# A hybrid decoder layer on one core: the delta rule's queries, keys and values turned by DMAs and VectorE instead of TensorE

## What is computed

```python
(gla_q, gla_k, gla_v, gla_lr, gla_r, gdn_qkv, gdn_b, gdn_a, gdn_z,
 xa_q, gate_logits) = jnp.split(u @ w_in, idx, axis=-1)
...
qkv = causal_short_conv(gdn_qkv, gdn_conv)      # 4 taps along the tokens, then SiLU
q, k, v = jnp.split(qkv, [GDN_QK, 2 * GDN_QK], axis=-1)
q = l2norm(q...) * (GDN_DK ** -0.5);  k = l2norm(k...)
o = gdn_chunked(q, k, v, g, beta)               # 8 heads of 128, chunks with a triangular solve
o = rmsnorm(o, gdn_norm) * jax.nn.silu(gdn_z...)
y_gdn = o @ w_up_gdn
```

## Time and profile before

| | |
|---|---|
| median of 3 runs (lowest to highest) | 2496.83 us (2495.46 to 2498.13) |
| the profiled execution | 2495.89 us, its span 2494.2 us |
| busy: PE, PEld, DVE, ACT, POOL | 99%, 82%, 56%, 50%, 17% |
| L676, the matmuls of the stream | 86% of the chain that ended last |
| DMA | 498.53 MB, 200 GB/s on the mean |
| `nat<-nat`, DMAs that exchange quarters | x416, 32 KB each, 3.7 us to landing |

### The profile page before, as it was taken

The page is one execution under the profiler, slowest core; times in us unless marked ns, Lnnn a source line. Parts: engine busy times, 40 slices in busy tenths (PEclk is TensorE's granted clock), DMA queues, the critical chain, the costliest instruction groups (busy, mean ns, idle before and its releaser), DMA issues.

```text
span 2494.2 us, 32008 instructions
## 1 busy us (share of the span) xinstructions
PE 2467.6 (99%) x11197; PEld 2044.4 (82%) x11197; DVE 1397.4 (56%) x1698; ACT 1235.8 (50%) x1502; POOL 430.8 (17%) x853
## 2 busy tenths in 40 slices
PE   9999999999999999999999999999999999999998
PEld 7888888888888888888888888888888888888887
DVE  5555555555556456676676564465655555555444
ACT  6444444444445456757585444444644444444443
POOL 6212121122101003223231120010121211211000
PEclk9999999999999999999999999999999999999999
DMA  7777677677768656555564766765676776767654
GB/s 251 211 201 210 202 208 203 202 214 210 215 211 266 195 171 171 167 161 163 158 178 135 215 207 196 225 221 187 215 211 200 204 206 201 210 201 252 194 190 157
DMA packets 305838, 498.53 MB, mean 200 GB/s; under 512 B 28236, under 2 KB 102096, under 8 KB 304976
## 3 DMA queue, kind: packets, MB, share of 16 engines
q1 hardware_dynamic: 282336, 457.85, 61.7%
q0 software_dynamic: 23120, 38.95, 4.9%
q10 hardware_dynamic: 288, 0.52, 0.1%
HBM read 471.39 MB, written 8.52 MB: 192 GB/s over the span
## 4 chain that ended last, share of the span: by engine, by line
PE 91%; POOL 2%; DVE 2%; DMA 2%; ACT 2%; issue 1%; SPq 0%; DVEq 0%; POOLq 0%; ACTq 0%
PE acc L676 86%; POOL mkh L636 1%; POOL mkh L639 1%; PE acc L718 1%; PE acc L701 1%; DMA post_a<-n_ffn_post 1%; DMA sq<-mk_scratch 1%; DVE wlo L1580 1%; ACT whi L1105 0%; DMA raw<-w_ffn_gu 0%; PE mix L736 0%; PE mix L945 0%; DMA raw<-w_in 0%; PE mix L839 0%; PE mix L979 0%
## 5 line engine op out<-in xcount | busy, mean ns | idle before, releaser
L1580 DVE TENSOR_TENSOR wlo<-raw,whi 128x1024 fp32r<-128x1024 f32 x860 | 1052.1, 1228 | 898.6 <-ACT whi L1105 895.3
L1105 ACT ACTIVATE whi<-raw 128x1024 fp32r<-128x1024 f32 x860 | 909.8, 1060 | 1177.2 <-PE acc L676 1134.7
L676 PE MATMUL acc<-whi,x_hi 128*128 128x512 f32 x1616 | 629.6, 390 | 0.0
L676 PE MATMUL acc<-whi,x_lo 128*128 128x512 f32 x1616 | 628.7, 389 | 0.0
L676 PE MATMUL acc<-wlo,x_hi 128*128 128x512 f32 x1616 | 628.7, 389 | 0.0
L676 PE MATMUL acc<-whi,u_hi 128*128 128x512 f32 x896 | 357.4, 399 | 1.9 <-ACT pr L1187 1.3
L676 PEld LDWEIGHTS acc<-whi,x_lo 128*128 128x128 f32 x1616 | 303.3, 188 | 63.2
L676 PEld LDWEIGHTS acc<-wlo,x_hi 128*128 128x128 f32 x1616 | 303.3, 188 | 62.7
L676 PEld LDWEIGHTS acc<-whi,x_hi 128*128 128x128 f32 x1616 | 303.3, 188 | 62.5
L300 POOL DMA_DIRECT2D nat<-nat x416 | 204.0, 498 | 848.4 <-DVE nat L1702 676.2
L676 PE MATMUL acc<-whi,u_lo 128*128 128x512 f32 x896 | 349.4, 390 | 0.0
(11 more groups left out here) (360 smaller groups left out, 1627.8 us busy)
## 6 DMA issues: line engine op xcount, KB each, us to landing
raw<-w_ffn_gu SPq DMA_DIRECT2D x352, 512.0 KB
raw<-w_ffn_down SPq DMA_DIRECT2D x176, 512.0 KB
raw<-w_in SPq DMA_DIRECT2D x224, 256.0 KB
raw<-w_in SPq DMA_DIRECT2D x96, 512.0 KB
raw<-w_mem_kv SPq DMA_DIRECT2D x32, 512.0 KB
raw<-w_out SPq DMA_DIRECT2D x32, 512.0 KB
nat<-nat POOLq DMA_DIRECT2D x416, 32.0 KB, 3.7
raw<-w_in SPq DMA_DIRECT2D x64, 128.0 KB
```

The costliest lines, as they stand in the source:

```text
L676: ins = nc.tensor.matmul(acc[:, par, t, :], x[:, k0 + k, cols], w[:, s, k, :], start=first and k == 0 and m == 0, stop=last and k == UK - ...
L1105: act(whi[:, s], raw[:, s], ACT.Copy).then_inc(hi_ready, 1)
L1580: tt(wlo[:, s], raw[:, s], whi[:, s].bitcast(fp32), ALU.subtract).then_inc(lo_ready, 1)
```

## The change

ScalarE now evicts chunks 0 and 1 by `take_in`: queries, keys and values go to `in_rows` with their columns in four quarters, in runs of 32 numbers; `z` goes to a place of its own (`z_in`, behind them in `pr`). For chunk 1 these are four instructions instead of two. GpSimd's new `swap_in(g)` waits for both evictions and exchanges quarters of partitions by 16 DMAs of 48 KB into `in_swapped`, which shares its place with `o_turned` and `o_swapped`. It is issued ahead of the loop for group 0 and at the end of the body for group g+1, behind the 30 instructions of the substitution. VectorE's new `turn_in(g)` in slot 25 waits for them and makes two block transposes of 128x768 into `x_in`, at the place of `in_rows`. The twelve transposes of L874 in each group are gone, with `gdn_in`; ScalarE seeds the convolution from `x_in` in SBUF, and VectorE's taps read `x_in` in SBUF instead of `mix` in PSUM. The evictions of the next chunks 0 and 1 wait for `conv_done`. TensorE's wait `groups_done` moves from step 0 to step 1.

```diff
+TURN_IN = STEP_AT.index(21)
...
+        flat = pr[:, 0:2, :, :].rearrange("p c t n -> p (c t n)")
+        in_rows, x_in = flat[:, 0:6 * SEQ], flat[:, 0:6 * SEQ].rearrange("p (k s) -> p k s", s=SEQ)
+        z_in = flat[:, 6 * SEQ:8 * SEQ].rearrange("p (t n) -> p t n", t=NT)
+        in_swapped = sums[:, :, :, :].rearrange("p c t n -> p (c t n)")[:, 0:6 * SEQ]
...
+            def swap_in(g):
+
+                for par in range(2):
+                    pl.wait_ge(acc_out[par], QB["proj"] // 2 + g * 2 + 1)
+                if g:
+                    pl.wait_ge(sem("in_turned"), g)
+                if g > 1:
+
+                    pl.wait_ge(sem("out_swapped"), 256 * (g - 1))
+                    pl.wait_ge(sem("out_lo"), g - 1)
+                for j in range(4):
+                    for q in range(4):
+                        pl.dma_start(in_swapped[32 * j:32 * j + 32, q * 384:(q + 1) * 384],
+                                     in_rows[32 * q:32 * q + 32, j * 384:(j + 1) * 384]).then_inc(sem("in_swapped"), 16)
+
+            swap_in(0)
             for g in range(NG):
...
                     pl.tensor_tensor(xcol[:, :, i + 1:], xcol[:, :, i + 1:], term[:, :, i + 1:], ALU.subtract).then_inc(sem("substituted"), 1)
+                if g + 1 < NG:
+                    swap_in(g + 1)
...
-                if j == 0:
+                if j == 1:
+
                     groups_done(pe, g)
-                    pe.wait_ge(acc_out[0], qp + g * 2 + 1)
-                    pe.wait_ge(acc_out[1], qp + g * 2 + 1)
-                    for b in range(3):
-                        for h in range(2):
-                            for t in range(NT):
-                                o = (b % 2) * 256 + h * P
-                                ins = nc.tensor.transpose(mix[:, b, h * SEQ + t * P:h * SEQ + (t + 1) * P],
-                                                          pr[:, b // 2, t, o:o + P], ident)
-                    ins.then_inc(sem("gdn_in"), 1)
...
+            def take_in(n, c):
+
+                ac.wait_ge(unit_used, n + 1)
+                v = in_rows.rearrange("p (j t k l) -> p t k j l", j=4, t=NT, l=32)
+                for t in range(NT):
+                    scale = rs[:, R_H1, t:t + 1]
+                    if c == 0:
+                        ins = act(v[:, t, 0:4], acc[:, 0, t, :].rearrange("p (k j l) -> p k j l", j=4, l=32), ACT.Copy, scale=scale)
+                    else:
+                        act(v[:, t, 4:6], acc[:, 1, t, 0:256].rearrange("p (k j l) -> p k j l", j=4, l=32), ACT.Copy, scale=scale)
+                        ins = act(z_in[:, t], acc[:, 1, t, 256:512], ACT.Copy, scale=scale)
+                ins.then_inc(acc_out[c], 1)
...
-                    need("gdn_in")
+                    need("in_turned")
...
-                            ins = act(conv[:, 2 * b + h, :], mix[:, b, h * SEQ:(h + 1) * SEQ], ACT.Copy,
+                            ins = act(conv[:, 2 * b + h, :], x_in[:, 2 * b + h, :], ACT.Copy,
...
-                    act(zg[:, :, :], pr[:, 1, :, 256:512], ACT.Silu)
+                    act(zg[:, :, :], z_in, ACT.Silu)
...
-                    for name in (("gdn_in",), ("gdn_in", "silu_zr"), ("gla_in", "gla_o"), ("xa_in", "silu_zr"))[c]:
+                    if c < 2:
+                        ac.wait_ge(sem("conv_done"), mixed * 3 + 3)
+                    for name in ((), ("silu_zr",), ("gla_in", "gla_o"), ("xa_in", "silu_zr"))[c]:
...
-                            ins = stt(y, mix[:, b, h * SEQ:(h + 1) * SEQ - s], cwg[:, 3 * (TAPS - 1 - s) + b, h:h + 1], y,
+                            ins = stt(y, x_in[:, 2 * b + h, 0:SEQ - s], cwg[:, 3 * (TAPS - 1 - s) + b, h:h + 1], y,
...
+            def turn_in(g):
+
+                ve.wait_ge(sem("in_swapped"), 256 * (g + 1))
+                src = in_swapped.rearrange("p (q t k l) -> p t k q l", q=4, t=NT, l=32)
+                dst = x_in.rearrange("p k (t q l) -> p t k q l", q=4, l=32)
+                for t in range(NT):
+                    ins = nc.vector.transpose(dst[:, t], src[:, t])
+                ins.then_inc(sem("in_turned"), 1)
...
+                    if j == TURN_IN:
+                        turn_in(g)
```

## The result

The changed kernel takes 2501.80 us, the median of 10 runs (2499.81 to 2502.82); ten runs of the kernel before on the same chip had a median of 2496.57 (2495.34 to 2498.33). The ratio is 1.0021, with a 95% interval of 1.0012 to 1.0029. I had forecast 2498.9, with a range up to 2501.5, which the result passes by 0.3 us: the change costs 5.2 us where I had 2.1 for its own effect. The interval lies above 1 as a whole: the changed kernel is slower, by some 0.2%. The profiled execution took 2500.99 us (span 2499.2) against 2495.89.

What follows compares the result with a forecast made beforehand. TensorE, busy 99%, sets the time, but GpSimd's `zbl` and VectorE's `sql` leave it hardly any room. Gain 0.58 and collisions 2.7 gave +2.1 us on 2495.89, plus 0.94 to the median: 2498.9 us, range 2494.2 to 2501.5.

Steps and rivals of the forecast that it cites:

- (e): TensorE's other steps, loads and substitution start move with TensorE's own time; the four waits at L945 stay 9.1 us.
- The collision: First conv taps, now reading SBUF, against GpSimd's products in groups 2 to 4: 0.83 + 0.95 + 0.95 = 2.7 us lost.
- The 0.12 us of room: Group 2's row sums at L907 start 0.20 us after `sql` and need 0.08, so 0.12 us of delay is absorbed.
- Rival 2: No exclusion between taps and GpSimd's products: only the 0.58 us gain, 2496.2 us, chance 0.25.
- Group 1: First mixer group, no step 24 ahead: ScalarE's seed and VectorE's chain to L907 come earlier, gain 0.58 us (0.4 to 1.31).
- rival 1: Taps collide with GpSimd's products as forecast: 2498.9 us, by its own bounds 2498.3 to 2499.8, chance 0.50.
- Groups 2 to 4 gain nothing: TensorE, 1.31 us earlier without transposes, waits 1.31 us more at L880 for GpSimd's `zbl`; gain nothing.
- rival 3: The whole 5.24 us of TensorE's transposes arrives as gain: 2491.6 us, chance 0.06.
- The new work: GpSimd's 16 DMAs, VectorE's two block transposes a group, ScalarE's runs of 32 and the `conv_done` wait: cost 0, covered.
- rival 5: DMAs not through by slot 25, so VectorE stands there and TensorE behind it: 2502 us or more, chance 0.04.
- rival 4: ScalarE's evictions in runs of 32 out of PSUM cost double, 3.2 us on top of the collision: 2502.1 us, chance 0.09.

Runs made afterwards that it cites:

- filled: Changed kernel and kernel before, each with ten useless matmuls on TensorE ahead of its wait for the substitution: 2498.48 and 2495.28 us.
- step 14 later: Changed kernel and kernel before, each with TensorE's use of the substitution nine matmuls later, inside its next unit: 2492.57 and 2490.07 us.
- the three pairs: Changed kernel against kernel before: as they are (2501.80, 2496.57 us), with the substitution wait filled (2498.48, 2495.28), with that step later (2492.57, 2490.07).
- Experiments 1 and 3: 1: changed kernel with twelve unread transposes a group back on TensorE, 2502.99 us; 3: kernel before with one transpose a group instead of twelve, 2496.22 us.
- experiment 7: Kernel before with ten useless matmuls on TensorE ahead of its wait for the substitution (L945): 2495.28 us.

## Why the prediction was wrong

**The step that failed is (e)**, "the 9.1 us of L945 stay". They stayed (9.0), but I read a wait as a cost that is fixed by its length. Behind a wait of 2.6 us (start to start) the granted clock fell to 1.2 GHz in some groups and not in others, at 1.6 us each. The changed kernel's profile has two falls, that of before none, and the medians of the two pairs without falls put the clock's share of the change at 2.0 (filled) to 2.7 us (step 14 later). I had quoted a clock of 1.00 from a stretch that has no such wait, and never looked at the stretches in which TensorE stands for longest once it has started up. A hint stood in the times: the profiled execution of the kernel before was 0.94 us faster than its median. I carried that along as a constant; it was an execution without a fall, with a median that has them.

**The collision: mechanism right, term low by 0.2 to 0.4 us.** Forecast 0.83 + 0.95 + 0.95 = 2.7. The taps lost 1.13 + 0.74 + 0.86 = 2.7, as forecast. But without falls the row sums came later by 1.17, 0.90 and 1.06 us with the wait filled, 3.1 in all, and by 1.09, 0.83 and 0.99 with step 14 later, 2.9 in all. The 0.12 us of room that I gave group 2 wasn't there, and the first tap starts 0.07 us later behind ScalarE's seed in each of the three groups, which I had left out there; a few hundredths of a us per group aren't settled. The Trainium skill, page "SBUF — State Buffer", section "Who interferes with whom", says that a VectorE instruction with two SBUF inputs and a GpSimd instruction that reads SBUF exclude each other; the traces agree, with 1.66 and 1.34 us for a tap of 0.48, and 480 ns again once GpSimd's products are elsewhere. Rival 2 (no exclusion) falls with that.

**Group 1: right.** Gain 0.58 forecast; 0.62, 0.58 and 0.62 us in the three pairs. (The range that I gave for rival 1, 2498.3 to 2499.8, should have been 2498.5 to 2499.9 by its own bounds; it makes no difference here.)

**Groups 2 to 4 gain nothing: right.** I wrote that the weight load's wait for `zbl` would grow from 0.3 to 1.6; the matmul waits 4.5 us in 3, up to 1.6. Experiments 1 and 3 show it from both sides, so rival 3 (the whole 5.24 us) is out.

**The new work: right but for 0.4 us.** The issues behind the substitution, the block transposes, and the split behind them, in group 1:

```profile
983.87 7.42 POOL L615 DMA_DIRECT2D sums<-pr  x15 [0.20 <-issue]
...
1007.96 1.83 DVE L2081 STREAM_TRANSPOSE pr<-sums 128x768 f32<-128x768 f32 x2
1010.21 1.23 DVE L1613 TENSOR_TENSOR wlo<-raw,whi 128x1024 fp32r<-128x1024 f32 x1 [0.42 <-ACT whi L1119]
```

Sixteen issues in some 8 us, no wait for `in_swapped`, 1.83 us of VectorE in a gap of 2.17, and 0.42 of it left: rival 5 is out. ScalarE's evictions in runs of 32 (the second row is chunk 0, the first what was left as it was):

```profile
L1201 ACT ACTIVATE pr<-acc,rs 128x512 f32<-128x512 f32 x16 | 10.0, 679 | 0.0
...
L1211 ACT ACTIVATE pr<-acc,rs 128x512 f32<-128x512 f32 x8 | 5.0, 682 | 0.0
```

682 ns against 679: rival 4 is out, although its time, 2502.1, is the one nearest to the measured 2501.8: that is chance. What I had not costed is 0.36 us at the end of the program, seen in each kernel that turns the inputs and in none that doesn't; what makes VectorE late there isn't settled.

**The sum as it stands now**: -0.6 (group 1) + 2.9 to 3.1 (collisions) + 0.4 (end) = 2.7 to 2.9, against 2.5 and 3.2 between the medians of the pairs without falls. The falls are what is left to 5.2, 2.0 to 2.7, and so not a separate measurement; the profiled pair, with two falls against none, has 3.2 of them. What isn't settled is which waits are followed by a fall. The seven profiles that have these waits hold 28 of them, all of 2.63 to 2.68 us from start to start; nine were followed by a fall. In one kernel it was groups 2 and 4, in another 1 and 3, and the runs of one kernel differ in it. That the changed kernel has more of them than the one before is measured; that it is so by more than the places at which its waits happen to lie is not shown.

## What to carry to other kernels

Work taken off the busiest engine comes back only from where nothing else is due at the same moment: look first for who releases it at the next two waiting points (here GpSimd's `zbl` and VectorE's `sql`), and if they are late, loosen those first. The largest cost in this kernel was neither the transposes nor their replacement but one wait of 2.3 us per group at a fixed place in TensorE's order, worth 6.6 us in the kernel before with the clock that fell behind it (1.3 of them by experiment 7): put the use of a late result some matmuls into the next block of work. And before an operand is moved from PSUM to SBUF, look at what GpSimd does at that moment.

## What the runs showed of the hardware that I had not expected

- A wait of TensorE of 2.6 us can be followed by a granted clock of 0.51 (starts 0.43 us apart for 0.23), 1.6 us a time, and by none in another group of the same execution. Ten useless matmuls in the gap made a kernel 3.3 us faster.
- The mean granted clock of a run tells it roughly without a profile: runs of the same kernel at 0.999 and 0.998 took 2495.3 and 2497.3 us on the mean, and the one at 0.997 took 2500.2.
- A VectorE product with a scalar pointer, `SCALAR_TENSOR_TENSOR`, costs the same out of PSUM and out of SBUF (476 and 480 ns) when it is alone, and out of SBUF up to 1.66 us beside a GpSimd product.
- An eviction that writes runs of 32 numbers costs what a plain one does (682 and 679 ns).
